# Sixteen pairs of gate tiles by seven half-width products each

## The reference

```
for l in range(DEPTH):                       # DEPTH = 2
    h = rmsnorm_2(x, pre_norm_g[l])
    proj = h @ w_in[l]
    (u, v, z_a, c_q, c_kv, k_rope, z_b, x_c, z_c,
     g_a, g_b, g_c) = jnp.split(proj, cuts, axis=-1)
    y_a = gmlp_spatial(u, v, ...) * jax.nn.silu(z_a)
    y_b = mla_attention(c_q, c_kv, k_rope, ...) * jax.nn.silu(z_b)
    y_c = rg_lru(x_c, ...) * jax.nn.silu(z_c)
    merged = (jax.nn.sigmoid(g_a) * (y_a @ w_proj_a[l])      # y_a, y_b: 1024 wide
              + jax.nn.sigmoid(g_b) * (y_b @ w_proj_b[l])
              + jax.nn.sigmoid(g_c) * (y_c @ w_proj_c[l]))   # y_c: 1280 wide
    x = x + rmsnorm_2(merged @ w_out[l], post_norm_g[l])
```

## Time and profile before

| | |
|---|---|
| Time, median of 3 runs | 3152.33 us (3152.31 to 3152.98) |
| Span of the profiled execution, first to last instruction | 3150.8 us |
| TensorE busy | 3140.4 us (100%), granted clock 1.000 |
| VectorE busy | 1859.9 us (59%) |
| ScalarE busy | 1258.6 us (40%) |
| POOL busy | 394.9 us (13%) |
| mean busy share of the 16 DMA engines | queue of the weights 32.1% |
| chain that ended last, by engine | PE 96%, DVE 3%, ACT 1% |

### The profile page before, as it was taken

The page is one execution under the profiler, slowest core; times in us unless marked ns, Lnnn a source line. Parts: engine busy times, 40 slices in busy tenths (PEclk is TensorE's granted clock), DMA queues, the critical chain, the costliest instruction groups (busy, mean ns, idle before and its releaser), DMA issues.

```text
span 3150.8 us, 36896 instructions
## 1 busy us (share of the span) xinstructions
PE 3140.4 (100%) x14840; PEld 2628.4 (83%) x14840; DVE 1859.9 (59%) x2504; ACT 1258.6 (40%) x1889; POOL 394.9 (13%) x287
## 2 busy tenths in 40 slices
PE   9999999999999999999999999999999999999999
PEld 8888888888888888888888888888888888888887
DVE  6876456665687655665557642447656754344754
ACT  4323334434433334443445422226635442223742
POOL 1201112110020121112012000110011100011001
PEclk9999999999999999999999999999999999999999
DMA  4332323235442223222642232223332222323432
GB/s 170 116 101 94 101 94 108 100 123 191 149 121 96 97 89 113 96 98 97 204 144 88 78 102 92 89 94 118 124 132 73 82 94 96 98 87 96 138 99 102
DMA packets 105354, 345.42 MB, mean 110 GB/s; under 512 B 13824, under 2 KB 14080, under 8 KB 104416
## 3 DMA queue, kind: packets, MB, share of 16 engines
q1 hardware_dynamic: 101856, 328.47, 32.1%
q0 software_dynamic: 3184, 14.06, 1.3%
q10 hardware_dynamic: 144, 0.52, 0.1%
HBM read 324.65 MB, written 2.10 MB: 104 GB/s over the span
## 4 chain that ended last, share of the span: by engine, by line
PE 96%; DVE 3%; ACT 1%; DMA 0%; SPq 0%; issue 0%; POOL 0%; POOLq 0%
PE ps L520 94%; DVE r L1484 1%; PE ps L611 1%; DVE wl L1474 1%; PE ps L852 0%; DVE f L1489 0%; SPq L2261 0%; DVE f L1552 0%; DMA X<-x_in 0%; DMA f<-f 0%; DVE r L1900 0%; DVE f L1722 0%; ACT wh L982 0%; ACT f L1308 0%; DVE sm L1921 0%; PE ps L564 0%
## 5 line engine op out<-in xcount | busy, mean ns | idle before, releaser
L520 PE MATMUL ps<-h,wh 128*128 128x512 f32 (+1 forms) x5824 | 1695.3, 375 | 0.7 <-DVE wl L1474 0.3
L520 PEld LDWEIGHTS ps<-h,wh 128*128 128x128 f32 x5824 | 1063.4, 188 | 200.1 <-issue 3.4
L520 PE MATMUL ps<-h,wl 128*128 128x512 f32 (+1 forms) x2912 | 1091.2, 375 | 0.0
L1474 DVE TENSOR_TENSOR wl<-raw,wh 128x1024 fp32r<-128x1024 f32 (+1 forms) x583 | 739.1, 1280 | 294.9 <-ACT wh L982 293.7
L982 ACT CAST wh<-raw 128x1024 fp32r<-128x1024 f32 (+2 forms) x596 | 592.3, 1006 | 685.9 <-PE ps L520 684.7
L520 PEld LDWEIGHTS ps<-h,wl 128*128 128x128 f32 x2912 | 547.1, 188 | 98.9
L520 PE MATMUL ps<-r,wh 128*128 128x512 f32 x1536 | 473.4, 389 | 0.9 <-DVE r L1484 0.5
L520 PEld LDWEIGHTS ps<-r,wh 128*128 128x128 f32 x1536 | 288.1, 188 | 62.2 <-issue 2.1
L1074 ACT CAST r<-f 128x512 fp32r<-128x512 f32 x194 | 119.8, 621 | 517.1 <-DVE f L1820 149.0
L520 PE MATMUL ps<-r,wl 128*128 128x512 f32 x792 | 304.3, 389 | 0.0
L520 PE MATMUL ps<-wh,r 128*128 128x512 f32 x960 | 302.4, 390 | 0.3
(11 more groups left out here) (160 smaller groups left out, 2133.5 us busy)
## 6 DMA issues: line engine op xcount, KB each, us to landing
raw<-wst SPq DMA_DIRECT2D x544, 512.0 KB, 3.3
raw<-wst SPq DMA_DIRECT2D x48, 320.0 KB, 3.0
r<-r SPq DMA_DIRECT2D x64, 128.0 KB, 2.3
f<-gains POOLq DMA_DIRECT2D x6, 1024.0 KB, 5.2
...
```

The costliest lines, as they stand in the source:

```text
L520: return e.matmul(o, a, b, start=start, stop=stop, skip_group_check=True)
L1474: e.tensor_tensor(l[:, 0:WIDTH[c]], raw[:, c % NRAW, 0:WIDTH[c]], h[:, 0:WIDTH[c]].bitcast(F32), ALU.subtract).then_inc(*lo_cut.up(("lo", c)))
```

## The change

In both layers of the second block, 16 pairs of neighbouring gate tiles (per layer `gateb_3`/4 and 5/6, and in a and c 2/3, 4/5 and 6/7) are computed together as a product of 2x2 blocks by seven products instead of eight. The blocks are 512 of the inner dimension, 128 output columns and 256 rows of `x`. A product is 4 slices by three matmuls of 128x256, so a pair takes 84 matmuls of 128x256 instead of 48 of 128x512.

The core of it, first the tables and the chunks. A pair's two raw chunks give four part chunks `*0` to `*3` (P0 to P3 below) of two halves each (P3 has one). Some of the halves are sums of quarters of the weights, which POOL makes in `sums`.

```diff
-AHEAD = {0: 1, 1: 1, 2: 1, "b": 1, "a": 1, "c": 2}
+AHEAD = {0: 1, 1: 1, 2: 1}
+
+
+PAIR_J = {"b": (3, 5), "a": (2, 4, 6), "c": (2, 4, 6)}
...
+PAIRS = [f"{L}/gate{nm}_{j}" for L in (2, 3) for nm in "bac" for j in PAIR_J[nm]]
+
+
+def places():
+
+    out, r = [], 0
+    while r < len(RAWS):
+        name = RAWS[r][0]
+        out += [(f"{name}*{q}", r, q) for q in range(4)] if name in PAIRS else [(name, r, None)]
+        r += 2 if name in PAIRS else 1
+    return out
+
...
+def released(r):
...
+    return ("sums", CHUNKS[c][0][:-2], 3), ("lo", c + 2)
...
+STEPS = {b: lambda one, two, after: (one, two, after and after + "*0", after and after + "*1") for b in "ba"}
+STEPS["c"] = lambda one, two, after: (one + "+", "", two, after + "*1" if after else two + "+")
+GATE_RING = {"b": (68, 47, 48, 46, 67), "a": (64, 65, 66, 67), "c": (64, 65, 66, 67)}
```

```diff
+            def two_tiles(L, name, between):
+
+                c = NAME[f"{name}*0"]
+                first, second, third = (take((name, i)) for i in "abc")
+                product(first, name, 0, 0, quarter(0, 0), True).then_inc(*group_done.up(("done", (name, "p1"))))
+                for m in "1643":
+                    w.wait_ge(*at("mixed_lo", L, m))
+                product(second, name, 0, 1, combined("1"), True).then_inc(*group_done.up(("done", (name, "n5")), ("closed", c)))
+                product(third, name, 1, 0, quarter(0, 1), True, True).then_inc(*group_done.up(("done", (name, "p2"))))
+                w.wait_ge(*at("copied", name, "p1"))
+                product(first, name, 1, 1, combined("6")).then_inc(*group_done.up(("done", (name, "u2")), ("closed", c + 1)))
+                w.wait_ge(*at("copied", name, "n5"))
+                product(second, name, 2, 0, combined("4"), False, True).then_inc(*group_done.up(("done", (name, "p3"))))
+                between(0)
+                w.wait_ge(*at("copied", name, "u2"))
+                product(first, name, 2, 1, combined("3")).then_inc(*group_done.up(("done", (name, "u3")), ("closed", c + 2)))
+                between(1)
+                w.wait_ge(*at("copied", name, "u3"))
+                product(first, name, 3, 0, quarter(1, 1), False, True).then_inc(
+                    *group_done.up(("done", (name, "c21")), ("closed", c + 3)))
+                between(2)
...
+                for n, j in enumerate(PAIR_J[b]):
+                    two_tiles(L, f"{L}/gate{b}_{j}", lambda i: some(2 * n + (i > 0), (whole, whole[:cut], whole[cut:])[i]))
+                if b == "b":
+                    tile(f"{L}/gateb_7", xs)
```

ACT's part. `kept` copies a half bank out of PSUM; `first`, `second` and `then` cut chunks by `STEPS`:

```diff
+            def two_gates(L, b, j, first, second, then):
+
+                name, lo, up = f"{L}/gate{b}_{j}", halves(0), halves(1)
+                g0, g1 = gate_at(L, b, j), gate_at(L, b, j + 1)
+
+                def kept(dst, i, what):
+                    w.wait_ge(*at("done", (name, what)))
+                    e.copy(dst, bank((name, i))[:, lo]).then_inc(*act_tile.up(("copied", name, what)))
+
+                w.wait_ge(*at(*gate_free(L, b, j)))
+                kept(g0[:, lo], "a", "p1")
+                kept(g0[:, up], "b", "n5")
+                first()
+                w.wait_ge(*at(*gate_free(L, b, j + 1)))
+                kept(g1[:, lo], "a", "u2")
+                w.wait_ge(*at("c11", name))
+                e.activation(g0[:, lo], g0[:, lo], ACT.Sigmoid).then_inc(*act_tile.up(("gate11", name)))
+                second()
+                kept(g1[:, up], "a", "u3")
+                then(0)
+                w.wait_ge(*at("c12", name))
+                w.wait_ge(*at("c22", name))
+                e.activation(g1, g1, ACT.Sigmoid).then_inc(*act_tile.up(("gate", L, b, j + 1)))
+                w.wait_ge(*at("done", (name, "c21")))
+                w.wait_ge(*at("c22", name))
+                e.activation(g0[:, up], bank((name, "a"))[:, lo], ACT.Sigmoid).then_inc(
+                    *act_tile.up(("gate", L, b, j), ("free", (name, "a"))))
+                then(1)
```

DVE's part, with the layer norm's steps, which leave `BESIDE`:

```diff
+            def two_gates(L, b, j, n, first, second, then):
+
+                name, lo, up = f"{L}/gate{b}_{j}", halves(0), halves(1)
+                g0, g1 = gate_at(L, b, j), gate_at(L, b, j + 1)
+                w.wait_ge(*at("done", (name, "p2")))
+                w.wait_ge(*at("copied", name, "p1"))
+                e.tensor_tensor(g0[:, lo], g0[:, lo], bank((name, "c"))[:, lo], ALU.add).then_inc(
+                    *dve_tile.up(("c11", name), ("free", (name, "c"))))
+                first()
+                w.wait_ge(*at("done", (name, "p3")))
+                w.wait_ge(*at("copied", name, "u2"))
+                e.tensor_tensor(g1[:, lo], bank((name, "b"))[:, lo], g1[:, lo], ALU.subtract).then_inc(
+                    *dve_tile.up(("c12", name), ("free", (name, "b"))))
+                second()
+                w.wait_ge(*at("copied", name, "u3"))
+                e.tensor_tensor(g1[:, up], g0[:, up], g1[:, up], ALU.subtract).then_inc(*dve_tile.up(("c22", name)))
+                then(0)
+                gated(L, b, 2 * n)
+                then(1)
+                gated(L, b, 2 * n + 1)
...
+                more = "+" if b == "c" else ""
+                for n, j in enumerate(PAIR_J[b]):
+                    name = f"{L}/gate{b}_{j}"
+                    after = f"{L}/gate{b}_{j + 2}" if n + 1 < len(PAIR_J[b]) else ""
+                    to(f"{name}*3")
+                    ahead = STEPS[b](f"{L}/pr{b}_{2 * n}", f"{L}/pr{b}_{2 * n + 1}", after)
+                    two_gates(L, b, j, n, lambda: to(ahead[0]), lambda: to(ahead[1]), lambda i: to(ahead[2 + i]))
+                    if after:
+                        to(f"{after}*2")
+                    if n:
+                        merged((2 * n - 2, 2 * n - 1))
+                    if b == "b":
+                        small_step("layer_norm", L, n)
+                if b == "b":
+                    slot(f"{L}/gateb_7")
+                for j in range(2 * len(PAIR_J[b]), 8):
+                    slot(f"{L}/pr{b}_{j}{more}")
+                    if j == 6:
+                        merged((4, 5))
+                    if b == "b" and j in (4, 5):
+                        small_step("layer_norm", L, j - 2)
+                    gated(L, b, j)
+                merged((6, 7))
```

More of the change, by code:

```diff
@@ L122, in proj, with gate, product @@
         def proj(nm, w, nk, b):
-            if nm != "b":
-                for j in range(AHEAD[nm]):
-                    one(f"gate{nm}_", D2["gate"] + 1024 * b, j)
-            for j in range(8):
-                if j < 8 - AHEAD[nm] and (nm != "b" or j > 1):
-                    one(f"gate{nm}_", D2["gate"] + 1024 * b, j + AHEAD[nm])
+            def gate(j):
+                one(f"gate{nm}_", D2["gate"] + 1024 * b, j)
+            def product(j):
                 if nk == 8:
@@ L133, in proj @@
                     out.append(fm(f"{L}/pr{nm}_{j}+", w, l, range(5, 10), rng(j * P)))
+            if nm != "b":
+                gate(0)
+                gate(1)
+            for n, j in enumerate(PAIR_J[nm]):
+                gate(j)
+                gate(j + 1)
+                product(2 * n)
+                product(2 * n + 1)
+            if nm == "b":
+                gate(7)
+            for j in range(2 * len(PAIR_J[nm]), 8):
+                product(j)
         for n in range(2):
@@ L683, in after, with gate_proj @@
                 early_second(B)
-            def gate_proj(L, b, g, p, ys, ready, first=0, kind="one"):
+            def gate_proj(L, b, g, p, ys, ready):
                 xs = pair(0, 8, 8)
                 n = AHEAD[b]
-                if first == 0:
-                    for j in range(n):
-                        tile(f"{L}/gate{g}_{j}", xs)
+                for j in range(n):
+                    tile(f"{L}/gate{g}_{j}", xs)
                 for j in range(8):
-                    if 1 < j <= first:
-                        banks.let_go(f"{L}/gate{g}_{j - 1}")
-                    if first <= j + n < 8:
+                    if j + n < 8:
@@ L696, in gate_proj @@
                         tile(f"{L}/gate{g}_{j + n}", xs)
                     key = ("pr", L, b, j)
[L698 to L701 removed]
+                    name = f"{L}/pr{p}_{j - j % 2}"
+                    if j % 2 == 0:
+                        slot(name)
+                    h, l = weights(name)
+                    o = take(key)
+                    for k in range(4):
+                        w.wait_ge(*at(*ready, k))
@@ new lines, in gate_proj, with product @@
+                    last = group(o, h, l, [(j % 2 * 4 + k) * P for k in range(4)], ys)
+                    closes = (("closed", NAME[name]),) if j % 2 else ()
+                    last.then_inc(*group_done.up(("done", key), *closes))
+            def product(o, name, q, second, xs, start=False, stop=False):
+                c = NAME[f"{name}*{q}"]
+                h, l = split_at(c)
+                w.wait_ge(*at("lo", c, second))
+                for k, (xh, xl) in enumerate(xs):
+                    col = second * S + k * P
```

(25 more changed lines are left out.)

370 lines of the change are left out of this document (260 added, 110 removed).

## The result

The changed kernel takes 3264.85 us (3263.42 to 3268.42, 4 runs) against 3152.32, a ratio of 1.0358 (1.0344 to 1.0373): 112.5 us slower. The direction was forecast; the size, +64, was not, and the time lies above the range.

What follows compares the result with a forecast made beforehand. It took the kernel as bound by TensorE's gapless stream of matmuls. Waits of 72.2 plus 8 for the clock less 15.8 of matmuls gave +64.4, a span of 3215.2 and a median of 3217 us, range 3190 to 3238.

Steps and rivals of the forecast that it cites:

- The ring in c: Branch c, four places for a pair's eight chunks: six PE waits of 2.34 us a layer before B and B+, 14.0.
- `gateb_7`: End of branch b: PE idles 6.8 us a layer for this tile's lo part, queued on DVE behind a layer norm step.
- `pra_6`: End of branch a: PE waits 2.2 us a layer for this tile's lo part, behind gated 5.
- A in b's second pair: Branch b, second pair: chunk A's lo part comes late behind DVE's queue, a PE wait of 1.9 us a layer.
- The clock: PE's slower pace after long waits: 2.0 us for each of four waits, 8 in all, nothing for other waits.
- four waits of 6.8: PE's waits of 6.8 us before `gateb_7` and before the fourth product of c's first pair, in both layers.
- third rival: In c, PE runs at its lower clock level after twelve ring waits, 1.7 us more each: +20, 3237 us; 11 in 100.
- What it adds on PE's path: Waits from queues at branch starts, lo parts behind other work and c's ring: 36.1 us a layer, 72.2 in both.
- What it adds beside other work: nothing: Attention heads: the mixtures' casts and subtractions fit in idle time of ACT, DVE and POOL, costing 0.
- b's first pair: Start of branch b: the fourth product waits 0.8 us a layer for ACT's copy of product 1.
- `prc_6`: End of branch c: PE waits 3.0 us a layer for this tile's lo part, behind gated 5 and two `m_lo`.
- What it removes: PE's matmuls: each pair costs 9.89 us where it cost 10.88, so 16 pairs save 15.8.

Runs made afterwards that it cites:

- e11: The changed kernel with c's ring reordered, branch ends cut ahead, mixtures later, banks kept, and c's start and small steps reordered: 3142.4 us, 0.9970 of the kernel before.
- e7: The changed kernel with dummy matmuls put ahead of most of PE's waits, about as long as the waits, to keep PE busy: 3242.4 us.
- e5: The changed kernel with POOL making the mixtures of h only behind the scores of attention head 1: 3251.4 us.
- e6: The changed kernel with b's first pair taking its three banks before those of gates 1 and 2 are let go: 3252.0 us.

## Why the prediction was wrong

- **What bounds it, and the direction: right.** Each wait that the order implied was in the trace at its place, but for the one at a's start (0 for 0.6). The ring in c was 27.9 in both layers for 28.0 forecast, which is partly luck: twelve waits of 2.04 would be 24.5, and POOL's sums made three of them longer by 3.5. The rest, `gateb_7` 13.1 for 13.6, `pra_6` 4.0 for 4.4, A in b's second pair 3.3 for 3.8.
- **The step that failed most: "The clock".** I allowed 2.0 for each of four waits of 6.8 and nothing for the others. e11 puts the change in busy time at full clock at -10.8; the changed kernel has +24.7, so the lower clock cost 35.5, not 8. The windows of 1 us give 33.1 of that directly; the other 2.4 are not settled. It follows waits of 2.0 and 3.3 as well, though not all of them. The price for the four long waits came true: within PE's busy time the windows show 2.0, 2.8, 1.4 and 1.7, 8.0 in all for the 8 forecast. That is luck in part, since the 2.0 came from the pace at the program's start and single drops differ from it. What failed is the nothing for all the other waits: 25.2 stand at the twelve other drops, at waits of 2.0 to 4.6. e7 shows the price by taking only the idle time away. My third rival ("The clock falls in c too") had the mechanism, for c alone, at 11 in 100 and +20.
- **Waits: 87.8 for 72.2.** Two things were missing in "What it adds on PE's path". One is that POOL's additions slow DVE: head 0 (+6.8 in both layers, shown by e5), and, by the timelines and not by a run of their own, c's start (+4.6) and three of the six waits before B (+3.5, which the shorter rest of the ring made up for). "What it adds beside other work: nothing" was wrong, since a cover in idle time does not cover a shared port. The other is b's first pair, where I followed the copy of product 1 but not the banks: 3.3 for 0.8, shown by e6. `prc_6` was 0.9 longer in each layer than worked out.
- **What it removes: 10.8 for 15.8.** At full clock a product of 12 narrow matmuls took 1.41 as forecast. The rest is in small pieces: in e11 1.4 us arose in the first 1640 us, to whose stream of matmuls the change adds nothing, and the switches between widths cost some 0.03 each. I did not settle it further.
- **The sum.** Clock 27.5, waits 15.6 and matmuls 5.0 more than forecast are 48.1, the difference between +112.5 and +64.4.
- **The range** took the ring, the queues and a dearer matmul in, but not the clock and the contention together, and both work in one direction.
